# The opening of a two-layer trunk: squares and split pieces dealt out anew, the second scale units moved into the first products, no products of zeros

## Chip, cores and metric

One core of a Trainium2 chip. The metric is the device time of one execution in microseconds (us), the median over runs. The kernel before takes 1187.4 us (three runs, 1187.0 to 1189.1).

## What is computed

A trunk of two layers over 256 latent tokens and 256 context tokens of width 1024. Layer 0 is attention beside a convolution module, layer 1 banded attention beside a state-space mixer, each followed by a gated feed-forward network. All norms are modulated by shifts and scales that are themselves a product with the condition vectors. The opening, which is what the change touches, is this part:

```python
sh1, sc1, g1, sh2, sc2, g2 = jnp.split((jax.nn.silu(c) @ mod_w[l] + mod_b[l])[:, None, :], 6, axis=-1)
csh1, csc1, ... = jnp.split(jax.nn.silu(c_ctx) @ mod_w[l] + mod_b[l], 6)
h  = modulate(rms_norm(x,  norm1_g[l]), sh1, sc1)      # h * (1 + scale) + shift
hc = modulate(rms_norm(cx, norm1_g[l]), csh1, csc1)
q, k, v, glu = jnp.split(h @ w_in, cuts, axis=-1)      # even_mixer, layer 0
```

## The kernel before

Activations stand feature-major in SBUF: `X[:, f, :]` is feature tile f (0 to 7) by 512 tokens. A product of fp32 accuracy is made of three: weights and activations are split in a high part that the fast format holds (`w_hi`, `Hhi`) and the rest (`w_lo`, `Hlo`), and hi x hi, hi x lo and lo x hi are summed. Each weight block (8 tiles by 256 columns, 1 MB) comes by SyncE's queue into one of four slots `raw`; ScalarE makes `w_hi`, VectorE `w_lo`, in two halves of 1024 columns, and a slot is free when both halves of `w_lo` are made (semaphore `lo_split`). The stream of loads is a list: blocks 0 and 1, four loads of the shifts of `mod_w` (0, 0, k=4 to 7), block 2, and so on; load r goes to slot r mod 4. So shift loads 4 and 5 have slots 2 and 3 at once, and shift loads 6 and 7 must wait until the halves 1 of blocks 0 and 1 are split. SyncE issues in the order of the list and stands at each wait.

The order of the opening is written out by hand, engine by engine:

TensorE (`@block.tensor`): fourteen products of zeros, `cvec` with itself, into a bank nobody reads (L2011). Then 32 transposes of x, four for each f (L2006), with three transposes of the small vectors `vrow` behind f=3. Then the sums of squares, `first_sum(f)`, four small products each (L2101), with `mod_unit(0)` behind f=3; `mod_unit(1)`; the turn of the first scales `scales_T(0)` and `spread_roots`, which spreads 1/rms over the partitions (L2117); `mod_unit(2)` and `mod_unit(3)` (L2039). Units 0 and 1 give the first four tiles of scales, 2 and 3 the second four; each is 16 products of a condition vector with a load `first_mod[m]`. Then `first_two()`: the first two weight blocks. `column(b, j, m)` is the three products of block b, feature tile j and output half m. It goes through block 0 with j=0 to 3, block 1 with j=0 to 3, the shift units `mod_unit(4)` to `mod_unit(7)` (L2055), block 0 with j=4 to 7, and the rest. The turn of the second scales, `scales_T(1)`, stands ahead of j=3 of block 0.

VectorE (`@block.vector`): `turned(f)` copies the transposed tile out of PSUM for even f (ScalarE does it for odd f, L749), `square0(f)` squares f = 0, 2, 4, 6 (L1214), the reciprocal of the root (L1368), `scales_copy(0)` (L1241), `first_gains(0)`, which makes the gains from the turned scales (L1248, L1251); then `gained0(f)`, the normed tile `n_h0` in two halves (L1377), `low0(f)`, its rest `Hlo` (L1384), and `first_lo(w, part)` (L660), a half of `w_lo`. `first_gains(1)` stands ahead of `first_lo(0, 1)` and `first_lo(1, 1)`, and `gained0` for f=4 to 7 needs those gains.

ScalarE: `turned` for odd f; `vec_ready`, then silu of the condition vectors into `cvec` (L757); a table load; `turned(5)`, `turned(7)`; the squares 5 and 7 (L764); the root (L786); `first_high(f)`, which is `Hhi` (L791), and `first_hi(w, part)` (L654).

GpSimd: the squares 1 and 3 (L698), then `w_hi` and `w_lo` of the first half of block 0 (L701, L703), then `Hlo` of f = 2, 4, 6 (L713). A tiny `ptap` memset (L710) passes on the count for the tiles that VectorE makes.

SyncE: x and the context, small vectors, then in order `first_block(0, 0)`, `first_scales(0)`, `(1)`, `first_block(1, 0)`, `first_scales(2)`, `(3)`, `first_block(0, 1)`, `first_block(1, 1)`, and the list. The loads 0 and 1 of the scales count on one semaphore, on which `mod_unit(0)` waits for both; 2 and 3 have one each.

Of the kernel before, what the change touches and what calls it, by code (L numbers as in the profile page):

```python
# [26 lines left out]
P = 128  # L27
# [129 lines left out]
def build_trunk(nc, a, out):  # L157
    with ExitStack() as ctx:
# [156 lines left out]
        def s(name):  # L315
            if name not in S:
                S[name] = sem(name)
            return S[name]
# [6 lines left out]
        def tiles(w):  # L325
            return w.rearrange("(k p) n -> p k n", p=P)
# [144 lines left out]
        def _(sp):  # L471
# [5 lines left out]
            def first_scales(i):  # L477

                rows_, cols_ = 4 * P * (i % 2), P * SC1 + 4 * P * (i // 2)
                sp.dma_start(first_mod[i][:, :].rearrange("p (k n) -> p k n", k=4),  # L480
                             tiles(a["mod_w"][0, rows_:rows_ + 4 * P, cols_:cols_ + 4 * P])).then_inc(s(f"scales_loaded{max(i - 1, 0)}"), 16)

            def first_block(r, part, loaded):

# [171 lines left out]
        def first_lo(w, part):  # L656

            c0 = 1024 * part
            nc.vector.wait_ge(hi_split, FIRST[w, part])
            nc.vector.tensor_tensor(w_lo[:, w, c0:c0 + 1024], raw[:, w, c0:c0 + 1024], w_hi[:, w, c0:c0 + 1024].bitcast(F32),  # L660
                                    ALU.subtract).then_inc(lo_split, 1)
# [5 lines left out]
            return Cc[:, i - 10, :], lambda tap: XB[:, i, 0, tap:tap + LAT]  # L667

        LOW_DVE = (0, 1, 3, 5, 7)
        SQ_DVE, SQ_POOL, SQ_ACT = (0, 2, 4, 6), (1, 3), (5, 7)  # L670
        XS_BANK = (p5, pmod, p5, pmod, p7, p5, pmod, p7)
        OUT_BANK = ((p5, p6), (p7, pmod))
        X_TOK = ((0, 0, p7), (0, 1, p5), (1, 0, p6), (1, 1, p7))
# [18 lines left out]
        @block.gpsimd  # L692
        def _(pool):
            nc.gpsimd.memset(U[:, :, :, :], 0.0).then_inc(s("pads_A"), 1)

            for i, f in enumerate(SQ_POOL):
                pool.wait_ge(s("xT_act"), f // 2 + 1)
                nc.gpsimd.tensor_tensor(sq0[:, f, :], X[:, f, :], X[:, f, :], ALU.mult).then_inc(s("sq_pool"), 1)  # L698

            pool.wait_ge(s("first_rows0"), 16)  # L700
            nc.gpsimd.tensor_copy(w_hi[:, 0, 0:1024], raw[:, 0, 0:1024]).then_inc(hi_split, 1)  # L701
            pool.wait_ge(hi_split, 1)
            nc.gpsimd.tensor_tensor(w_lo[:, 0, 0:1024], raw[:, 0, 0:1024], w_hi[:, 0, 0:1024].bitcast(F32), ALU.subtract)\  # L703
                .then_inc(lo_split, 1)

            for f in range(KD):
                if f in LOW_DVE:

                    pool.wait_ge(s("h_lo_dve"), LOW_DVE.index(f) + 1)
                    nc.gpsimd.memset(ptap[:, f:f + 1], 0.0).then_inc(s("h_lo"), 1)  # L710
                    continue
                pool.wait_ge(s("h_hi"), f + 1)
                nc.gpsimd.tensor_tensor(Hlo[:, f, :], n_h0[:, f, :], Hhi[:, f, :].bitcast(F32), ALU.subtract)\  # L713
                    .then_inc(s("h_lo"), 1)

            pool.wait_ge(s("h_lo"), 3 * KD)
            nc.gpsimd.memset(XB[:, :, :, 0:2], 0.0).then_inc(s("pads_C"), 1)
            nc.gpsimd.memset(XB[:, :, :, 2 + LAT:4 + LAT], 0.0).then_inc(s("pads_C"), 1)
            pool.wait_ge(s("pads_C"), 2)
            pool.wait_ge(s("aux_done"), 6)  # L720
            nc.gpsimd.memset(Xb[:, 4:6, 2 * LAT:2 * T], 0.0).then_inc(s("parts_zero"), 1)
# [3 lines left out]
        def _(act):  # L725
# [34 lines left out]
            turned(5)  # L760
            turned(7)
            for f in SQ_ACT:
                act.wait_ge(s("xT_act"), f // 2 + 1)
                A(sq0[:, f, :], X[:, f, :], ACT.Square).then_inc(s("sq_ready"), 1)  # L764

            def root(n, t):
# [432 lines left out]
        def _(dve):  # L1199
# [11 lines left out]
            def square0(f):  # L1211

                dve.wait_ge(s("xT_dve"), f // 2 + 1)
                V_.tensor_tensor(sq0[:, f, :], X[:, f, :], X[:, f, :], ALU.mult).then_inc(s("sq_dve"), 1)  # L1214
# [8 lines left out]
            square0(2)  # L1223
            turned(6)
            square0(4)
            square0(6)

            GROUPS = [(l, j) for l in range(DEPTH) for j in range(3)]

# [8 lines left out]
            def scales_copy(i):  # L1238

                dve.wait_ge(mod_used, 2 * i + 2)  # L1240
                V_.tensor_copy(modc[:, 0:P], pmod[:, 0:P]).then_inc(s("modc_ready"), 1)  # L1241
# [139 lines left out]
            def low0(f):  # L1381

                dve.wait_ge(s("h_hi"), f + 1)
                V_.tensor_tensor(Hlo[:, f, :], n_h0[:, f, :], Hhi[:, f, :].bitcast(F32), ALU.subtract)\  # L1384
                    .then_inc(s("h_lo_dve"), 1)
# [3 lines left out]
            low0(0)  # L1389
            gained0(2)  # L1390
            low0(1)
            scales_copy(1)
            gained0(3)
            dve.wait_ge(lo_split, 1)
            first_lo(1, 0)
            low0(3)
            first_gains(1)
            first_lo(0, 1)
            first_lo(1, 1)
# [601 lines left out]
        def _(pe):  # L2001
# [4 lines left out]
                return nc.tensor.transpose(o, x, cst("ident", 0, n, 0, n))  # L2006


            pe.wait_ge(s("cvec_zero"), 2)
            for _ in range(14):  # L2010
                mm(p6[0:32, 0:KD * 32], cvec[:, 0, :], cvec[:, :, :].rearrange("p k c -> p (k c)"), start=True, stop=True)  # L2011

            pe.wait_ge(s("const_loaded"), 16)
            pe.wait_ge(s("x_loaded"), 32)
            for f in range(KD):
# [11 lines left out]
            def mod_unit(m):  # L2027

                n, k = m // KD, m % KD
                if m < 4:  # L2030
                    pe.wait_ge(s(f"scales_loaded{max(m - 1, 0)}"), 32 if m < 2 else 16)
                    if m == 0:
                        pe.wait_ge(s("cvec_ready"), 1)
                    if m == 2:
                        pe.wait_ge(s("gains_ready"), 1)
                    for kk in range(4 * (m % 2), 4 * (m % 2) + 4):
                        for g in range(4):
                            c0 = 4 * P * (kk % 4) + P * g
                            ins = mm(pmod[32 * g:32 * g + 32, 0:P], cvec[:, kk, :], first_mod[m][:, c0:c0 + P],  # L2039
                                     start=(kk == 0), stop=(kk == KD - 1))  # L2040
                    ins.then_inc(mod_used, 1)
                    return
                r = m_raw[m]
                pe.wait_ge(raw_loaded[r % RAW_SLOTS], 16 * (r // RAW_SLOTS + 1))
                if k == 0 and n:
                    pe.wait_ge(s("mod_ready"), n)
                if k == 0 and n == 1:
                    pe.wait_ge(s("shift_ready"), 1)
                if n == 0:
                    if k == 4:  # L2050
                        pe.wait_ge(s("mod_ready"), 1)
                    for kk in range(2 * (k % 4), 2 * (k % 4) + 2):
                        for g in range(4):
                            c0 = D * (kk % 2) + 256 * g
                            ins = mm(pmod[32 * g:32 * g + 32, 0:256], cvec[:, kk, :], raw[:, r % RAW_SLOTS, c0:c0 + 256],  # L2055
                                     start=(kk == 0), stop=(kk == KD - 1))
                    ins.then_inc(mod_used, 1)
                    return
                if k == 0 and n == 3:
                    pe.wait_ge(s("yn_ready"), BT)  # L2060
                if k == 0 and n == 5:
                    pe.wait_ge(s("decay_ready"), 16)
                if k == 4 and n == 5:
                    pe.wait_ge(s("mod_ready"), 6)
                if n == 5:
                    for kk in range(2 * (k % 4), 2 * (k % 4) + 2):
                        for g in range(4):
                            c0 = D * (kk % 2) + 256 * g
                            ins = mm(pmod[32 * g:32 * g + 32, 0:256], cvec[:, kk, :], raw[:, r % RAW_SLOTS, c0:c0 + 256],
                                     start=(kk == 0), stop=(kk == KD - 1))  # L2070
                else:
                    for g in range(4):
                        ins = mm(pmod[32 * g:32 * g + 32, :], cvec[:, k, :], raw[:, r % RAW_SLOTS, g * 512:(g + 1) * 512],  # L2073
                                 start=(k == 0), stop=(k == KD - 1))
                ins.then_inc(mod_used, 1)
# [8 lines left out]
            def scales_T(i):  # L2084

                pe.wait_ge(s("modc_ready"), i + 1)
                T_(pmod[:, 0:P], modc[:, 0:P]).then_inc(s("modT_done"), 1)
# [37 lines left out]
            mod_unit(1)  # L2125
            scales_T(0)
            spread_roots(0, T)
            mod_unit(2)
            mod_unit(3)

            def part_ready(w, part, it=None, per=0):

# [43 lines left out]
            def first_two():  # L2176
# [11 lines left out]
                pe.wait_ge(lo_split, FIRST[0, 0])  # L2188
                for j in range(4):
                    pe.wait_ge(s("h_lo_dve") if j < 2 else s("h_lo"), j + 1)  # L2190
                    if j == 3:
                        scales_T(1)
                    for m in range(2):
                        column(0, j, m)
                pe.wait_ge(lo_split, FIRST[1, 0])
                for j in range(4):
                    for m in range(2):
                        ins = column(1, j, m)
                ins.then_inc(s("h_used"), 1)
# [785 lines left out]
```

## Time and profile before

| | |
|---|---|
| median of 3 runs | 1187.4 us (1187.0 to 1189.1) |
| profiled execution | 1187.6 us |
| its span | 1185.8 us |
| TensorE busy | 1157.7 us, 98% |
| VectorE busy | 693.6 us, 58% |
| ScalarE busy | 485.3 us, 41% |
| GpSimd busy | 13.9 us, 1% |
| chain that ended last | PE 85%, DVE 10%, ACT 2%, DMA 2% |

Times in the rows are us from the start of the span. PE is TensorE, PEld its weight loads, DVE VectorE, ACT ScalarE, POOL GpSimd, SP SyncE; SPq is SyncE's queue while it issues. In a row of the timeline the bracket at the end is the idle time ahead of the piece and who ended it. Matmuls overlap: a record of TensorE is longer than the distance to the next. A product of the first blocks counts as one record, a small fp32 product as two.

### The profile page before, as it was taken

The page shows a single profiled execution, that of the slowest core. Times are in us where ns is not written, and L with a number is a line of the kernel's source. Part 1 is how long each engine was busy: PE and PEld are TensorE (multiplying, and loading weights), DVE is VectorE, ACT ScalarE, POOL GpSimd, SP SyncE. Part 2 cuts the span into 40 slices and gives each one's busy share as a digit, 9 for nine tenths or more (in the row PEclk, how much of TensorE's full clock was granted, in tenths as well). Part 3 has the DMA queues.
Part 4 walks back from the last instruction along what each step waited for, and adds up shares of the span by engine and source line. Part 5 has one row for each costly group of instructions (what it writes and reads, how often), then busy time and mean ns, then how long its engine had stood idle before and what let it go on. Part 6 is the DMA issues. An engine that isn't in the chain of part 4 may idle for free.

```text
span 1185.8 us, 17766 instructions
## 1 busy us (share of the span) xinstructions
PE 1157.7 (98%) x7266; PEld 934.1 (79%) x7266; DVE 693.6 (58%) x1159; ACT 485.3 (41%) x744; POOL 13.9 (1%) x20
## 2 busy tenths in 40 slices
PE   8999999999999999999999999999999999999998
PEld 5777766777588888888887767899565898998997
DVE  5699978853643334423323368887789645554455
ACT  3423336552433232222212242367268636443442
POOL 3000000000000000000000000000000000000000
PEclk9999999999999999999999999999999999999999
DMA  9845473125543222332123664344140157655551
GB/s 346 316 152 177 159 251 122 36 82 203 184 139 104 88 76 84 125 123 84 67 80 116 206 198 142 95 119 143 36 143 2 47 178 239 213 177 179 193 167 65
DMA packets 118893, 167.73 MB, mean 141 GB/s; under 512 B 4797, under 2 KB 102695, under 8 KB 114599
## 3 DMA queue, kind: packets, MB, share of 16 engines
q1 hardware_dynamic: 118390, 166.23, 42.1%
q8 instruction: 50, 0.82, 0.3%
q10 hardware_dynamic: 433, 0.51, 0.2%
q14 instruction: 20, 0.16, 0.0%
HBM read 164.37 MB, written 1.05 MB: 139 GB/s over the span
## 4 chain that ended last, share of the span: by engine, by line
PE 85%; DVE 10%; ACT 2%; DMA 2%; issue 1%; SPq 0%; DVEq 0%; ACTq 0%; POOL 0%
PE acc L2153 20%; PE acc L2154 20%; PE acc L2155 20%; PE pmod L2073 2%; PE acc L2232 2%; PE acc L2233 1%; PE acc L2234 1%; PE p L2518 1%; PE p L2519 1%; PE p L2517 1%; DMA first_mod<-in_mod_w 1%; PE p L2006 1%; DVE Y L1429 1%; DVE sm L1511 1%; PE p L2395 1%
## 5 line engine op out<-in xcount | busy, mean ns | idle before, releaser
L646 DVE TENSOR_TENSOR w_lo<-raw,w_hi 128x1024 fp32r<-128x1024 f32 x222 | 249.0, 1163 | 234.8 <-ACT w_hi L636 234.5
L636 ACT ACTIVATE w_hi<-raw 128x1024 fp32r<-128x1024 f32 (+1 forms) x224 | 212.8, 998 | 408.7 <-PE acc L2155 358.2
L2153 PE MATMUL acc<-Hhi,w_hi 128*128 128x512 f32 (+1 forms) x960 | 326.3, 340 | 1.6 <-DVE w_lo L646 1.6
L2155 PE MATMUL acc<-Hhi,w_lo 128*128 128x512 f32 (+1 forms) x960 | 324.3, 338 | 0.0
L2154 PE MATMUL acc<-Hlo,w_hi 128*128 128x512 f32 (+1 forms) x960 | 324.2, 338 | 0.0
L2153 PEld LDWEIGHTS acc<-Hhi,w_hi 128*128 128x128 f32 x960 | 182.1, 190 | 25.7 <-issue 3.9
L2155 PEld LDWEIGHTS acc<-Hhi,w_lo 128*128 128x128 f32 x960 | 182.1, 190 | 19.6
L2154 PEld LDWEIGHTS acc<-Hlo,w_hi 128*128 128x128 f32 x960 | 182.2, 190 | 19.2
L2153 PE MATMUL acc<-hid_hi,w_hi 128*128 128x512 f32 x248 | 97.9, 395 | 0.1
L2154 PE MATMUL acc<-hid_lo,w_hi 128*128 128x512 f32 x248 | 96.6, 390 | 0.0
L2155 PE MATMUL acc<-hid_hi,w_lo 128*128 128x512 f32 x248 | 96.6, 389 | 0.0
L1429 DVE SCALAR_TENSOR_TENSOR Y<-U,vec,Y 128x512 f32<-128x512 f32 x120 | 82.0, 746 | 0.3
L1654 DVE TENSOR_TENSOR f_h<-acc,f_gate 128x1024 f32<-128x1024 f32 (+1 forms) x22 | 21.1, 958 | 102.2 <-PE acc L2155 100.2
L2153 PEld LDWEIGHTS acc<-hid_hi,w_hi 128*128 128x128 f32 x248 | 46.5, 188 | 13.9 <-issue 3.5
L2155 PEld LDWEIGHTS acc<-hid_hi,w_lo 128*128 128x128 f32 x248 | 46.6, 188 | 9.9
L2154 PEld LDWEIGHTS acc<-hid_lo,w_hi 128*128 128x128 f32 x248 | 46.6, 188 | 9.2
L1608 DVE SCALAR_TENSOR_TENSOR X<-acc,mod,X 128x256 f32<-128x256 f32 (+1 forms) x52 | 22.0, 478 | 40.5 <-PE acc L2155 40.5
L2232 PE MATMUL acc<-Hhi,w_hi 128*128 128x512 f32 (+1 forms) x96 | 35.4, 369 | 2.1 <-DVE Hlo L1353 2.1
L2153 PE MATMUL acc<-mixC_hi,w_hi 128*128 128x256 f32 x128 | 36.7, 287 | 0.0
L2154 PE MATMUL acc<-mixC_lo,w_hi 128*128 128x256 f32 x128 | 36.2, 283 | 0.0
L2155 PE MATMUL acc<-mixC_hi,w_lo 128*128 128x256 f32 x128 | 36.2, 283 | 0.0
L2073 PE MATMUL pmod<-raw,cvec 128*32 128x512 f32 x256 | 33.2, 602 | 1.2 <-DVE small L1327 1.2
(392 smaller groups left out, 1602.8 us busy)
## 6 DMA issues: line engine op xcount, KB each, us to landing
raw<-in_mod_w SPq DMA_DIRECT2D x44, 1024.0 KB, 5.3
raw<-in_ffn_w_in SPq DMA_DIRECT2D x44, 1024.0 KB, 5.1
raw<-in_od_w_in SPq DMA_DIRECT2D x15, 1024.0 KB, 5.4
raw<-in_ffn_w_out SPq DMA_DIRECT2D x12, 768.0 KB, 4.5
raw<-in_ev_w_in SPq DMA_DIRECT2D x8, 1024.0 KB, 7.5
raw<-in_od_w_out SPq DMA_DIRECT2D x8, 1024.0 KB, 5.9
raw<-in_ffn_w_out SPq DMA_DIRECT2D x8, 1024.0 KB, 5.0
raw<-in_ev_w_out SPq DMA_DIRECT2D x8, 768.0 KB, 6.3
```

The source lines that it names most:

```text
L636: nc.scalar.activation(w_hi[:, w % 2, c0:c1], raw[:, r % RAW_SLOTS, c0:c1], ACT.Copy)\
L646: nc.vector.tensor_tensor(w_lo[:, w % 2, c0:c1], raw[:, r % RAW_SLOTS, c0:c1], w_hi[:, w % 2, c0:c1].bitcast(F32), ALU.subtract).then_inc( ...
L1429: ins = V_.scalar_tensor_tensor(out=y, in0=U[:, i, :, tap:tap + LAT], scalar=col, in1=y, op0=ALU.mult, op1=ALU.add)
L1511: top = step.mark(V_.reduce_max(sm[:, v % 3, 0:1], sbank[v % 3][:, nk_of(v)[0] * P:T], AX.X))
L1608: ins = V_.scalar_tensor_tensor(out=xs, in0=src, scalar=gt, in1=xs, op0=ALU.mult, op1=ALU.add)
L1654: V_.tensor_tensor(f_h[:, :, 0:t], acc[:, 2:4, 0:t], f_gate[:, :, 0:t], ALU.mult)\
L2006: return nc.tensor.transpose(o, x, cst("ident", 0, n, 0, n))
L2073: ins = mm(pmod[32 * g:32 * g + 32, :], cvec[:, k, :], raw[:, r % RAW_SLOTS, g * 512:(g + 1) * 512], start=(k == 0), stop=(k == KD - 1))
L2153: mm(outs[m], hi[:, j, cols], xh, start=(first and j == 0), stop=False)
L2154: mm(outs[m], hi[:, j, cols], xl, start=False, stop=False)
L2155: ins = mm(outs[m], lo[:, j, cols], xh, start=False, stop=(last and j == kts - 1))
L2232: mm(o, hi[:, j, cols], xh, start=(j == 0), stop=False)
```

## The change

Seven edits, all in the opening:

1. The fourteen products of zeros are gone.
2. The square of f=6 moves from VectorE to ScalarE, between 5 and 7.
3. GpSimd makes only `w_hi` of the first half of block 0; `w_lo` of it, `first_lo(0, 0)`, goes to VectorE, into the place of the square of f=6. VectorE's wait for GpSimd's piece ahead of `first_lo(1, 0)` goes with it.
4. Scale loads 0 and 1 get a semaphore each, 2 and 3 share one; `mod_unit(0)` waits only for load 0, units 2 and 3 for both of theirs.
5. `mod_unit(2)` and `mod_unit(3)` move from ahead of `first_two()` to ahead of j=2 of block 0.
6. `scales_T(1)` moves from ahead of j=3 of block 0 to ahead of j=1 of block 1.
7. `scales_copy(1)` on VectorE moves from ahead of `gained0(3)` to behind `low0(3)`.

```diff
@@ first_scales
-  ... .then_inc(s(f"scales_loaded{max(i - 1, 0)}"), 16)
+  ... .then_inc(s(f"scales_loaded{min(i, 2)}"), 16)
@@
-        SQ_DVE, SQ_POOL, SQ_ACT = (0, 2, 4, 6), (1, 3), (5, 7)
+        SQ_DVE, SQ_POOL, SQ_ACT = (0, 2, 4), (1, 3), (5, 6, 7)
@@ GpSimd
             nc.gpsimd.tensor_copy(w_hi[:, 0, 0:1024], raw[:, 0, 0:1024]).then_inc(hi_split, 1)
-            pool.wait_ge(hi_split, 1)
-            nc.gpsimd.tensor_tensor(w_lo[:, 0, 0:1024], raw[:, 0, 0:1024], w_hi[:, 0, 0:1024].bitcast(F32), ALU.subtract)\
-                .then_inc(lo_split, 1)
@@ ScalarE
             for f in SQ_ACT:
-                act.wait_ge(s("xT_act"), f // 2 + 1)
+                act.wait_ge(s("xT_act") if f % 2 else s("xT_dve"), f // 2 + 1)
@@ VectorE
             square0(4)
-            square0(6)
+            first_lo(0, 0)
@@
             low0(1)
-            scales_copy(1)
             gained0(3)
-            dve.wait_ge(lo_split, 1)
             first_lo(1, 0)
             low0(3)
+            scales_copy(1)
             first_gains(1)
             first_lo(0, 1)
             first_lo(1, 1)
@@ TensorE
-            pe.wait_ge(s("cvec_zero"), 2)
-            for _ in range(14):
-                mm(p6[0:32, 0:KD * 32], cvec[:, 0, :], cvec[:, :, :].rearrange("p k c -> p (k c)"), start=True, stop=True)
@@ mod_unit
-                    pe.wait_ge(s(f"scales_loaded{max(m - 1, 0)}"), 32 if m < 2 else 16)
+                    pe.wait_ge(s(f"scales_loaded{min(m, 2)}"), 16 if m < 2 else 32)
@@
             spread_roots(0, T)
-            mod_unit(2)
-            mod_unit(3)
@@ first_two
                 for j in range(4):
                     pe.wait_ge(s("h_lo_dve") if j < 2 else s("h_lo"), j + 1)
-                    if j == 3:
-                        scales_T(1)
+                    if j == 2:
+                        mod_unit(2)
+                        mod_unit(3)
                     for m in range(2):
                         column(0, j, m)
                 pe.wait_ge(lo_split, FIRST[1, 0])
                 for j in range(4):
+                    if j == 1:
+                        scales_T(1)
                     for m in range(2):
                         ins = column(1, j, m)
```

TensorE's order from the second scale unit to the first products, before (`first_mod_90` to `_92` are the loads of units 1 to 3, `acc` the first products, `Hhi` and `w_hi` their high parts):

```order
L2101 MATMUL p<-sq_93,const 32x128 x16
L2039 MATMUL pmod<-first_mod_90,cvec 32x128 x16
L2006 MATMUL pmod<-const,modc 128x128
L2117 MATMUL p<-rs_95,const 128x128 x4
L2039 MATMUL pmod<-first_mod_91,cvec 32x128 x16
L2039 MATMUL pmod<-first_mod_92,cvec 32x128 x16
L2184 MATMUL acc<-Hhi,w_hi 128x512
```

The same place in the changed kernel:

```order
L2092 MATMUL p<-sq_93,const 32x128 x16
L2030 MATMUL pmod<-first_mod_90,cvec 32x128 x16
L2001 MATMUL pmod<-const,modc 128x128
L2108 MATMUL p<-rs_95,const 128x128 x4
L2173 MATMUL acc<-Hhi,w_hi 128x512
```

The two units stand twelve products further down, and the next `pmod<-const,modc` (the turn of the second scales) thirty products and the two units behind the first `acc`, where before it was eighteen products behind it.

VectorE's order from the first products' second tile to the tiles from 4 on, before, with what each row waits for:

```order
L1384 TENSOR_TENSOR Hlo<-n_h_76,Hhi 128x512 [waits h_hi]
L1241 COPY modc<-pmod 128x128 [waits mod_used]
L1377 SCALAR_TENSOR_TENSOR n_h_76<-X,gain,p 128x256 x2
L660 TENSOR_TENSOR w_lo<-raw,w_hi 128x1024 [waits hi_split,lo_split]
L1384 TENSOR_TENSOR Hlo<-n_h_76,Hhi 128x512 [waits h_hi]
L1248 TENSOR_TENSOR mod<-pmod,vec 128x8 [waits modT_done]
L1251 SCALAR_TENSOR_TENSOR gain<-mod,vec 128x8 [waits dve_step]
L660 TENSOR_TENSOR w_lo<-raw,w_hi 128x1024 [waits hi_split,mod_ready]
L660 TENSOR_TENSOR w_lo<-raw,w_hi 128x1024 [waits hi_split]
```

And in the changed kernel:

```order
L1380 TENSOR_TENSOR Hlo<-n_h_76,Hhi 128x512 [waits h_hi]
L1373 SCALAR_TENSOR_TENSOR n_h_76<-X,gain,p 128x256 x2
L660 TENSOR_TENSOR w_lo<-raw,w_hi 128x1024 [waits hi_split]
L1380 TENSOR_TENSOR Hlo<-n_h_76,Hhi 128x512 [waits h_hi]
L1237 COPY modc<-pmod 128x128 [waits mod_used]
L1244 TENSOR_TENSOR mod<-pmod,vec 128x8 [waits modT_done]
L1247 SCALAR_TENSOR_TENSOR gain<-mod,vec 128x8 [waits dve_step]
L660 TENSOR_TENSOR w_lo<-raw,w_hi 128x1024 [waits hi_split,mod_ready]
L660 TENSOR_TENSOR w_lo<-raw,w_hi 128x1024 [waits hi_split]
```

The copy of the second scales now stands directly ahead of the gains made from them; the last two `w_lo` are behind both, as before.

## Rows read from the trace of the kernel before

**Rows 1.** The page, busy time of TensorE over the whole span.

```profile
PE 1157.7 (98%) x7266; PEld 934.1 (79%) x7266; DVE 693.6 (58%) x1159; ACT 485.3 (41%) x744; POOL 13.9 (1%) x20
```

**Rows 2.** Chain of waits, 0 to 43 us: start, length, what.

```profile
24.20 1.66 DVE n_h L1377 x4
25.85 0.61 DVE Hlo L1384
...
31.25 0.34 PE pmod L2006
...
32.02 2.37 DVE w_lo L660 x2
34.41 6.80 DMA raw<-in_mod_w
...
41.24 1.07 PE pmod L2055 x16
...
43.21 0.23 PE acc L2184
```

**Rows 3.** Timeline of TensorE: start, length, instructions, pause ahead of them.

```profile
1.24 8.03 PE L2011 MATMUL p<-cvec 128*32 128x256 f32 x28 [1.24 <-DVE cvec L1205]
10.17 1.94 PE L2006 MATMUL acc<-const,xin 128*128 128x128 f32 x16 [0.91 <-DMA xin<-in_ctx]
...
16.08 0.64 PE L2101 MATMUL p<-sq,const 128*32 128x128 f32 x16 [1.10 <-DVE sq L1214]
17.95 1.39 PE L2039 MATMUL pmod<-first_mod,cvec 128*32 128x128 f32 x32 [1.23 <-DMA first_mod<-in_mod_w]
...
25.66 1.08 PE L2039 MATMUL pmod<-first_mod,cvec 128*32 128x128 f32 x32 [0.57 <-DMA first_mod<-in_mod_w]
...
38.34 3.98 PE L2055 MATMUL pmod<-raw,cvec 128*32 128x256 f32 x64
```

**Rows 4.** SyncE's waits, and the landings of its four shift loads (L517).

```profile
SPq L517 <- DVE w_lo L660: 11.2, 2, 10.4
DMA to landing us min/median/max: 5.4/9.1/12.4
```

**Rows 5.** Groups of TensorE from 1.2 to 5 us, and from 5 to 9.3.

```profile
L2011 PE MATMUL p<-cvec 128*32 128x256 f32 x9 | 3.9, 621 | 1.2 <-DVE cvec L1205 1.2
L2011 PE MATMUL p<-cvec 128*32 128x256 f32 x20 | 4.6, 386 | 0.0
```

**Rows 6.** Timeline of VectorE, 11 to 20 us.

```profile
11.71 0.69 DVE L1209 COPY X<-acc 128x512 f32<-128x512 f32 x1 [0.18 <-PE acc L2006]
...
13.52 0.52 DVE L1220 COPY vec<-p 128x364 f32<-128x364 f32 x1
...
15.15 0.87 DVE L1214 TENSOR_TENSOR sq<-X 128x512 f32<-128x512 f32 x1
...
16.55 2.86 DVE L1214 TENSOR_TENSOR sq<-X 128x512 f32<-128x512 f32 x2
```

**Rows 7.** Timeline of ScalarE, 14 to 22 us.

```profile
14.08 0.22 ACT L757 ACTIVATE cvec<-vec 128x16 f32<-128x16 f32 x1 [1.34 <-DVE vec L1220]
...
16.82 1.15 ACT L764 ACTIVATE sq<-X 128x512 f32<-128x512 f32 x2
21.10 0.37 ACT L786 ACTIVATE rt<-p,small 128x128 f32<-128x128 f32 x1 [3.13 <-PE p L2101]
```

**Rows 8.** Timeline of GpSimd, 15 to 30 us.

```profile
15.56 2.69 POOL L703 TENSOR_TENSOR w_lo<-raw,w_hi 128x1024 fp32r<-128x1024 f32 x1
...
28.07 1.29 POOL L713 TENSOR_TENSOR Hlo<-n_h,Hhi 128x512 fp32r<-128x512 f32 x1
```

**Rows 9.** Stretches: from:to, length, TensorE busy, granted clock, DMA share, GB/s.

```profile
15.00:18.60 3.60, 1.29 (x40) 1.00 1.07 371
18.60:22.00 3.40, 3.40 (x72) 0.50 1.05 385
32.50:33.00 0.50, 0.50 (x4) 1.00 0.12 49
```

More of the change, by code:

```diff
@@ L480, in first_scales @@
                 sp.dma_start(first_mod[i][:, :].rearrange("p (k n) -> p k n", k=4),
-                             tiles(a["mod_w"][0, rows_:rows_ + 4 * P, cols_:cols_ + 4 * P])).then_inc(s(f"scales_loaded{max(i - 1, 0)}"), 16)
+                             tiles(a["mod_w"][0, rows_:rows_ + 4 * P, cols_:cols_ + 4 * P])).then_inc(s(f"scales_loaded{min(i, 2)}"), 16)
             def first_block(r, part, loaded):
```

## The prediction

> **What bounds the kernel now.** I read the page first: of a span of 1185.8 us TensorE is busy 98% [rows 1]. So the whole program is one long TensorE queue, and a change in the opening matters by how far it moves the moment from which that queue no longer starves. The chain of waits for the first 43 us says what that moment hangs on [rows 2]. It reaches back to the loads of the first scales, for which TensorE waits until 17.95 [rows 3]; then come four sums of squares, the second unit, the copy and the turn of the scales, and at 24.20 VectorE makes the first `n_h`. From there the chain stays on VectorE until the turn of the second scales at 31.25, goes on with the last two halves of `w_lo` (32.02 to 34.39), and these free the slots of the raw ring: the transfer issued at 34.41 lands 6.80 later, and the last shift unit runs from 41.24 to 42.31. Behind that TensorE follows without a gap, a product each 0.23. So two things set the time at which the opening ends: TensorE's own work, and the last transfer, which waits for VectorE. TensorE's queue in order of time shows them nearly level, since the four shift units run 38.34 to 42.32, four times about one us, with no room for a wait [rows 3]. SyncE's queue shows the other side: it waited 11.2 us for exactly those two `w_lo` pieces [rows 4].
>
> **The change, part by part.** Times are of the profiled execution, 1187.6 us (span 1185.8 and 1.8 around it), 0.2 over the median of the three runs, 1187.4; I add the difference to the median.
>
> *No products of zeros.* They end at 9.27 and TensorE's first transpose waits for x until 10.17 anyway [rows 3], so no time of theirs is on the path. What they bought is the clock. The first nine of them take 3.76 us (1.24 to 5.0), 0.42 each; the next twenty take 4.3, 0.21 each [rows 5]. The engine's clock thus rose from 1.2 to 2.4 GHz at about 5 us, after 3.8 us of back-to-back work. In the changed kernel the transposes are the first work, so they meet the lower clock. The rule behind it is in the Trainium skill, "TensorE: Matmul & The Clock Gate", section "What's actually happening": the throttled state is the default and activity releases it; the first rows of zeros agree.
> Sixteen transposes take 1.94 at full clock [rows 3], 0.11 each with 0.16 for the tail; at half clock 0.22. The tile of f=2 is then turned at 10.17 + 12 x 0.22 + 0.16 = 12.97, VectorE copies it (0.69) and squares f=0 (0.87 at least), and copies `vec` after that, starting at about 14.7 where it was 13.52 [rows 6]. ScalarE's silu of `cvec` waits for that copy: 15.2 for 14.08 [rows 7]. Behind it stand, in ScalarE's order, a table load, two copies and the squares; from silu to the end of its two squares took 3.89 (14.08 to 17.97).
>
> *Sixth square on ScalarE.* A third square adds 0.57 there: 15.24 + 3.89 + 0.57 = 19.7. On VectorE the square of f=4 ends near 18.5 and the moved `first_lo(0, 0)` near 19.7. For the squares I take 0.87, the duration of the one at 15.15, and not the 1.43 of the two at 16.55: those ran beside GpSimd's subtraction of 15.56 to 18.25, which is removed [rows 6, 8]. The Trainium skill, "SBUF — State Buffer", on which operations grab the shared pair, says that a VectorE operation with two inputs in SBUF contends with GpSimd's reads; the longer squares agree. At the contended durations VectorE would be free about 0.2 later than the root needs it, and the sum would be larger by that 0.2. I keep ScalarE as the later one.
> The last sum then ends at about 20.1, for 21.05. From the root (21.10) to the first `n_h` (24.20) is 3.10 [rows 2, 7]. The second scale unit fits: 20.1 + 1.08 is before the reciprocal ends. So `n_h` starts at 20.15 + 3.10 = 23.25: a **gain of 0.95**. Its bounds: no cost of the low clock at all, 18.95 + 0.05 + 3.10 = 22.1, a gain of 2.1; low clock through the sums, the turn and the spreading of the roots (0.5 + 0.4 + 1.0 more), a loss of 0.9.
>
> *The splitting of the wait on the two scale loads* lets unit 0 start before 17.95. It stands ahead of sums that wait for later squares, so I cost it at nothing; its cover is ScalarE's squares up to 19.7.
>
> *Second scale units behind the second tile.* In the kernel before the second of them ran from 25.66 to 26.74, and the first ahead of it, while TensorE would have had nothing to do but wait for `Hlo` until 26.46 [rows 2, 3]. Now they stand in the dense part: 1.08 + 0.84, say 1.9 for the pair. Worse is what they push back, the turn of the second scales. Counted from the start of `n_h`: the first tile product can start at +2.26 (26.46 - 24.20); j=2 waits 0.15 for GpSimd's subtraction (28.07 + 1.29 = 29.36, +5.16 for +5.02) [rows 8]; the turn now has ahead of it j=0 to 3 of block 0 and j=0 of block 1, five times six products at 0.23 = 6.9, and the pair, 1.9. It is issued at +11.2, where it was at +7.05 (31.25): **4.15 later**, less the gain of 0.95, **3.2 later**, at 34.45. VectorE stands in `first_gains(1)` for it, doing nothing from about 29.5, with `first_lo(0, 1)` and `first_lo(1, 1)` queued behind, both of which had their input long before. SyncE waits for those with the two loads of the ring, and the DMA engines have been idle since about 32 (0.12 busy from 32.5 on) [rows 9]. So the second load is issued at 34.41 + 3.2 = 37.6 and lands at 44.4; unit 7 ends near 45.5 where it ended at 42.31. VectorE's later squares of work (`n_h` 4 to 7, Hlo) move by the same 3.2 and stay ahead of it. TensorE's own sum is smaller: 23.25 + 2.26 + 0.15 + 1.9 + 0.33 + 8 x 1.38 + 4 x 1.0 = 42.9, only 0.6 late; what decides is the load. TensorE reaches unit 6 at 40.9, finds its load landed at about 33.24 + 3.2 + 5.4 = 41.8 (5.4 is the shortest of the four landings [rows 4]), and then waits 1.6 for unit 7.
>
> *The clock once more.* Units 2 and 3 no longer fill TensorE's pause before the first tile: after the roots are spread (23.25) it has nothing until `Hlo` at 25.5, and it had a pause before the turn as well. From 15.0 to 18.6 TensorE was busy 1.29, in short pieces between pauses of 1.10 and 1.23, and at 18.65 the clock fell to 1.2 GHz for 3.4 us, until 22.06 [rows 3, 9]. The new pauses are of that kind: 1.1 ahead of the first turn (20.9 to 22.0), 1.3 of work, and 2.2 ahead of the first tile. A fall costs half of what it covers of dense products, at most 1.7, about **1.4** with the part that lies in the pause. The second pause, around units 6 and 7, can do the same.
>
> Sum: 3.2 + 1.4 = 4.6, nothing being absorbed later: up to 58 us TensorE has no pause, and its waits behind that are for VectorE and ScalarE work that moves along. **1187.4 + 4.6 = 1192.0 us.**
>
> **The rivals.** (a) The clock holds: only the load is late, 1187.4 + 3.2 = 1190.6. For it: after 22.06 the clock held over the pause of 0.57 ahead of unit 3 [rows 3]. (b) The clock falls at both pauses: 3.2 + 1.4 + 1.6 = 6.2, 1193.6. For it: around units 6 and 7 TensorE is busy only 2 in 4.6 us. (c) The head gains its full 2.1, because ScalarE's chain isn't held by the low clock: the turn is late by 4.15 - 2.1 = 2.05, and 1189.5 comes out. Against it: `vec` stands behind nineteen transposes. (d) The other side: the load is no longer the bound, at the place where unit 7 waits. TensorE's own sum decides then, and with a gain of 2.1 it is 0.6 - 1.15 = -0.55: 1186.9 or a bit less. It decides from the point where the last load takes less than 4.3 us (issued at 36.45, wanted at 40.8). Against it: the same load took 6.80, and none of the four under 5.4. (e) The change does nothing, since the scales were late by a transfer anyway: the chain has no transfer between 17.95 and 34.41, so this gets nearly nothing; it would be 1187.4.
>
> **How the numbers follow.** A measurement of this kernel tells about 0.2% (2.4 us) from no change. My case with one fall 0.36, (a) 0.20, (b) 0.17: these are slower by more than 0.2%, 0.73 together. (c) 0.14 and (e), with a part of the delay absorbed in a way I don't see, 0.06: within 0.2%, 0.20. (d) and gains I don't see, 0.07. The likeliest gives 1192.0. The range goes from 1188.4, which takes in (c) with a little absorbed, to 1194.4, (b) with 0.8 for a gain near nothing.
>
> **What would show it.** In the changed profile: the transposes at twice 0.11 each; silu near 15.2; three squares on ScalarE ending near 19.7; the first `n_h` near 23.2; VectorE idle about 5 us in front of the second `first_gains`, with the turn near 34.5; SyncE's wait for `w_lo` up from 11.2 to 14 or so; a transfer issued near 37.6 and TensorE waiting for it before unit 7; first tile products twice as long for up to 3.4 us if the clock falls. The prediction is wrong if unit 7 ends before 44, or if something behind 60 us gives time back.

## The result and the profile after

| | before | changed |
|---|---|---|
| median | 1187.52 us (6 runs, 1186.73 to 1189.1) | 1192.76 us (6 runs, 1192.06 to 1193.56) |
| profiled execution | 1187.6 us | 1192.4 us |
| its span | 1185.8 us | 1190.6 us |

The changed kernel takes 1.0044 of the time before, 95% interval 1.0031 to 1.0057: 5.2 us more by the medians, 4.8 by the profiled executions. The forecast was 1192.0.

The page, busy time by engine. It answers to [rows 1]: TensorE is busy 5.9 less, and its span is 4.8 longer.

```profile
PE 1151.8 (97%) x7238; PEld 932.9 (78%) x7238; DVE 692.4 (58%) x1159; ACT 485.9 (41%) x745; POOL 10.8 (1%) x19
```

The chain of waits of the changed kernel, 20 to 47 us (start, length, what), against [rows 2]:

```profile
20.18 0.38 ACT rt L782
20.58 0.95 DVE rs L1364
...
23.07 1.66 DVE n_h L1373 x4
...
29.91 1.98 PE pmod L2030 x64
36.21 0.12 PE pmod L2001
36.36 0.18 DVE mod L1244
...
36.76 2.37 DVE w_lo L660 x2
39.15 6.90 DMA raw<-in_mod_w
46.09 1.07 PE pmod L2046 x16
```

`n_h` starts 1.13 earlier (23.07 for 24.20). Between it and the turn of the second scales the chain has another path: before, it stayed on VectorE up to the turn at 31.25 [rows 2]; now, behind the first `Hlo`, it runs over TensorE's own products and the pair of units. From the turn on the members and their order are the same. `w_lo` starts 4.74 later (36.76 for 32.02), the transfer behind it is issued at 39.15 for 34.41, also 4.74 later, and unit 7 ends at 47.16 for 42.31, 4.85 late. The spans differ by 4.8, so nearly all of the loss is made in the 13 us between the first `n_h` and the second gains, and none of it is given back later.

TensorE's timeline of the changed kernel (start, length, instructions, and the pause ahead of them), against [rows 3]:

```profile
10.37 3.65 PE L2001 MATMUL acc<-const,xin 128*128 128x128 f32 x16 [10.37 <-DMA xin<-in_ctx]
...
29.84 2.05 PE L2030 MATMUL pmod<-first_mod,cvec 128*32 128x128 f32 x64
36.05 0.27 PE L2001 MATMUL pmod<-const,modc 128*128 128x128 f32 x1
40.38 1.93 PE L2046 MATMUL pmod<-raw,cvec 128*32 128x256 f32 x32
43.19 1.07 PE L2046 MATMUL pmod<-raw,cvec 128*32 128x256 f32 x16 [0.88 <-DMA raw<-in_mod_w]
46.09 1.07 PE L2046 MATMUL pmod<-raw,cvec 128*32 128x256 f32 x16 [1.83 <-DMA raw<-in_mod_w]
```

The four shift units, one row of 3.98 before, are now three pieces with two pauses for loads between them. The pauses stand where TensorE's queue touches the ring; read alone, they would say "the memory is slow". VectorE's timeline says whose fault they are:

```profile
29.23 0.68 DVE L1380 TENSOR_TENSOR Hlo<-n_h,Hhi 128x512 fp32r<-128x512 f32 x1
31.97 0.29 DVE L1237 COPY modc<-pmod 128x128 f32<-128x128 f32 x1 [2.06 <-PE pmod L2030]
36.36 0.17 DVE L1244 TENSOR_TENSOR mod<-pmod,vec 128x8 f32<-128x8 f32 x1 [4.10 <-PE pmod L2001]
```

Between `low0(3)` and the second gains VectorE is idle for 2.06 and 4.10 us, with two `w_lo` pieces queued behind that need nothing from either wait. SyncE's waits (engine, line, total us, times, longest), against the 11.2 of [rows 4]:

```profile
SPq L517 <- DVE w_lo L660: 15.3, 2, 14.5
```

And the stretches (from:to, length, TensorE busy, granted clock, DMA share, GB/s), for the clock, against [rows 9]:

```profile
23.00:26.50 3.50, 1.02 (x5) 1.00 1.08 359
26.50:30.00 3.50, 3.50 (x13) 0.53 1.04 407
42.00:45.50 3.50, 1.38 (x24) 1.00 1.00 382
46.50:50.00 3.50, 3.50 (x28) 1.00 1.09 411
```

Behind the pause ahead of the first tile the clock is at 1.2 GHz from 26.7 to 30.1: 13 records in 3.5 us of dense products. Behind the pauses at units 6 and 7 it holds in this execution.

### The profile page after: what moved, and what is told of

It reads as the page before. It is cut to its first block, busy times and chain, and to the rows that moved or that the text cites. A ratio compares the mean times of both kernels' runs of the same rounds, so it can differ in the third digit from the quotient of the medians.

```text
span 1190.6 us, 17708 instructions
## 1 busy us (share of the span) xinstructions
PE 1151.8 (97%) x7238; PEld 932.9 (78%) x7238; DVE 692.4 (58%) x1159; ACT 485.9 (41%) x745; POOL 10.8 (1%) x19
## 4 chain that ended last, share of the span: by engine, by line
PE 86%; DVE 9%; ACT 2%; DMA 1%; issue 1%; SPq 0%; DVEq 0%; ACTq 0%
PE acc L2142 20%; PE acc L2144 20%; PE acc L2143 20%; PE pmod L2064 2%; PE acc L2224 2%; PE acc L2226 1%; PE acc L2225 1%; PE p L2511 1%; PE p L2509 1%; PE p L2510 1%; PE acc L2001 1%; PE p L2001 1%; DVE Y L1424 1%; DVE sm L1506 1%; DMA xin<-in_ctx 1%
```

## The experiments

My theory at this point: 3.3 us come from the late transfers, which wait for VectorE, which waits for the turn; 1.5 from the fall of the clock in the pause ahead of the first tile. Rivals: TensorE's own sum with the units in the dense part decides (the loads don't matter), or the missing zeros and ScalarE's third square cost time themselves. Each comparison below is with the kernel before on the same chip, whose median lay between 1187.4 and 1188.1.

### The late halves of `w_lo` ahead of the wait

```diff
             low0(3)
+            first_lo(0, 1)
+            first_lo(1, 1)
             scales_copy(1)
             first_gains(1)
-            first_lo(0, 1)
-            first_lo(1, 1)
```

> The changed kernel with the last two halves of w_lo ahead of the copy and the gains of the second scales on VectorE, so that they no longer wait for the turn at 36.05. If the late transfers decide, SyncE issues them near 31 and 32, they land before TensorE asks, the two pauses ahead of units 6 and 7 (0.88 and 1.83) go, unit 7 ends near 44.4 instead of 47.16, and the time is 1192.8 - 2.8 = 1190.0 us. If TensorE's own work and its clock decide instead, it stays within 0.5 us of 1192.8.

Measured: 1189.68 us (10 runs), 1.0012 of before, interval 1.0002 to 1.0021. The first row is VectorE's timeline, the second TensorE's:

```profile
29.76 2.35 DVE L660 TENSOR_TENSOR w_lo<-raw,w_hi 128x1024 fp32r<-128x1024 f32 x2
```

```profile
40.41 3.66 PE L2046 MATMUL pmod<-raw,cvec 128*32 128x256 f32 x64
```

The pieces are made at 29.8 for 36.8, the shift units are one row again, and unit 7 ends at 44.07 for 47.16, though the turn itself is where it was (36.08). By the medians the excess over the kernel before is 1.6 where it was 5.2. So 3.1 us (unit 7 in the traces) to 3.7 (the excesses) were the late transfers, and TensorE's own sum isn't what decided in the changed kernel.

### The turn itself earlier

```diff
@@ first_two, in the changed kernel
                     if j == 2:
                         mod_unit(2)
                         mod_unit(3)
+                    if j == 3:
+                        scales_T(1)
@@ block 1
-                    if j == 1:
-                        scales_T(1)
```

> The changed kernel with the turn of the second scales ahead of j=3 of block 0, directly behind units 2 and 3 and one tile, instead of ahead of j=1 of block 1. If the place of the turn is what delays the last two loads, the turn is 2.8 earlier (33.3), both pauses at units 6 and 7 go, and the time falls by 2.5 to 3 us against the changed kernel, to the kernel before plus 2 to 2.5; the units themselves may stay where they are. If the units' place is what costs, the time stays at plus 4.5 to 5.

Measured: 1189.73 us (10 runs), 1.0018 of before (1.0008 to 1.0027), plus 1.9. The turn came at 34.50 and not at 33.3, because the clock stayed low for 6.8 us in this execution, but both pauses at the units are gone:

```profile
34.50 0.27 PE L2001 MATMUL pmod<-const,modc 128*128 128x128 f32 x1
41.52 3.82 PE L2046 MATMUL pmod<-raw,cvec 128*32 128x256 f32 x64
```

Two different edits, one on VectorE and one on TensorE, cut the same chain and end at the same 1189.7. What they have in common is that the last loads are issued in time. That the medians agree so closely is partly chance: unit 7 ended at 45.34 here and at 44.07 in the run before, since the clock was low for longer, and that run had another fall of the clock later on (last section).

### TensorE's pause filled

```diff
             spread_roots(0, T)
+            for _ in range(5):
+                mm(p7[0:32, 0:KD * 32], cvec[:, 0, :], cvec[:, :, :].rearrange("p k c -> p (k c)"), start=True, stop=True)
```

> The changed kernel with five idle products of cvec, as large as the products of zeros, between the spreading of the roots and the first tile; their result is read by nobody. If the pause there lets the clock fall, the granted clock now stays at 2.4 GHz from 26 to 31 and the turn is 1.5 earlier, near 34.6: 1191.2 us. If the fall has another cause, 1192.8 or a little more.

Measured: 1192.67 us (4 runs, 1190.79 to 1193.69), 1.0044 of before (1.0027 to 1.006). The profiled execution is the 1190.79 one; its stretches:

```profile
23.00:26.50 3.50, 3.25 (x15) 1.00 1.09 362
26.50:30.00 3.50, 3.50 (x73) 1.00 1.05 408
```

In the trace it is as expected: the clock stays at 2.4 GHz, 73 records in the second stretch where the changed kernel has 13, the turn at 34.38 for 36.05, and the span 1189.0 for 1190.6. The other three executions were 1.4 to 2.9 us longer, and the median does not move. The pauses of 0.88 and 1.85 at units 6 and 7 are still in this kernel. Their mean granted clock was lower, 0.997 to 0.999 for the 1.000 of the profiled one, and the slower the execution, the lower it was. So the clock was low for longer in them; in which place isn't shown, since there is no trace of them.

### Both mends

```diff
@@ VectorE
             low0(3)
+            first_lo(0, 1)
+            first_lo(1, 1)
             scales_copy(1)
             first_gains(1)
-            first_lo(0, 1)
-            first_lo(1, 1)
@@ TensorE
             spread_roots(0, T)
+            for _ in range(5):
+                mm(p7[0:32, 0:KD * 32], cvec[:, 0, :], cvec[:, :, :].rearrange("p k c -> p (k c)"), start=True, stop=True)
```

> The changed kernel with both mends: the last two halves of w_lo ahead of the copy and gains, and five idle products in the pause ahead of the first tile. If late loads and the fall of the clock are the whole of the loss and add up, the first takes 2.8 and the second 1.5 of it, and the kernel before plus 0.3 to 0.8 us is left, which is the 1.9 of the pair of units less the gain of the head. If a third cause is left, plus 1.5 or more.

Measured: 1187.58 us (11 runs, 1187.3 to 1188.2), 0.9999 of before (0.999 to 1.0008). Expected were 0.3 to 0.8 over before, which the interval still takes in; a third cause of 1.5 or more is excluded. So the two causes together make up the loss, within about 1 us. Part of the difference between -0.2 and the expected 0.3 to 0.8 can be the clock: eight of the eleven executions had a mean granted clock of 1.000, but only eight of the 21 of the kernel before, and between these two groups of eight the kernel with both mends is slower, 1187.5 for 1187.1 in the mean. In TensorE's timeline the whole of it can be seen, with no pause in the units, and unit 7 ending at 42.39 where it ended at 42.31:

```profile
22.76 2.35 PE L2120 MATMUL p<-cvec 128*32 128x256 f32 x10
28.30 1.96 PE L2030 MATMUL pmod<-first_mod,cvec 128*32 128x128 f32 x64
34.40 0.27 PE L2001 MATMUL pmod<-const,modc 128*128 128x128 f32 x1
38.73 3.66 PE L2046 MATMUL pmod<-raw,cvec 128*32 128x256 f32 x64
```

Without the mend of the pause the excess over before was 1.6, and here it is -0.2, so the pause costs 1.8 by the medians, about one fall of the clock; by the ends of unit 7 it is 1.68 (44.07 and 42.39).

### The move alone, and the zeros alone

```diff
@@ the kernel before
             spread_roots(0, T)
-            mod_unit(2)
-            mod_unit(3)
@@ first_two
-                    if j == 3:
-                        scales_T(1)
+                    if j == 2:
+                        mod_unit(2)
+                        mod_unit(3)
@@ block 1
+                    if j == 1:
+                        scales_T(1)
@@ VectorE
-            scales_copy(1)
             gained0(3)
             dve.wait_ge(lo_split, 1)
             first_lo(1, 0)
             low0(3)
+            scales_copy(1)
```

> The kernel before with nothing but the move of units 2 and 3, of the turn and of the copy of the second scales; zeros, squares, GpSimd's piece and the semaphores as before. If the move is the cause by itself, the first tile stays near 26.5, the turn is 4.3 to 5.8 late (35.5, or 37 where the clock falls in the pause from 24.1 to 26.5), TensorE waits ahead of units 6 and 7, and the time is the kernel before plus 4.3 to 7 us. If the head's edits are the cause, plus less than 1.

Measured: 1196.71 us (4 runs), 1.008 of before (1.0064 to 1.0095), plus 9.3: more than the upper end of what I expected. Its timeline of TensorE and a stretch:

```profile
40.48 1.93 PE L2055 MATMUL pmod<-raw,cvec 128*32 128x256 f32 x32
43.35 1.07 PE L2055 MATMUL pmod<-raw,cvec 128*32 128x256 f32 x16 [0.93 <-DMA raw<-in_mod_w]
47.11 1.93 PE L2055 MATMUL pmod<-raw,cvec 128*32 128x256 f32 x16 [2.69 <-DMA raw<-in_mod_w]
```

```profile
45.50:49.00 3.50, 1.89 (x17) 0.61 1.10 392
49.00:52.50 3.50, 3.50 (x12) 0.50 1.01 420
```

The turn was at 36.17, inside the expected 35.5 to 37, and the last load was issued at 39.27. But it took 7.80 to land, not 6.80, and the clock fell in the pause of 2.69, so that unit 7 and what follows ran at 1.2 GHz until about 53. Ahead of the first tile, on the other hand, TensorE had a pause of 2.52 here too, and the clock held:

```profile
23.00:26.50 3.50, 1.22 (x9) 1.00 1.09 361
26.50:30.00 3.50, 2.87 (x12) 1.00 1.03 403
```

So this is not rival (b) as it was written, with a fall at both pauses, but its second fall alone. The move by itself costs 4 us more than the whole change. That is not because the other edits had won 4: the head gained 1.65 (first `n_h` at 24.72 here, 23.07 in the changed kernel), which the fall in the first pause took back, so that the turn came at 36.17 and 36.05. The rest is made behind the turn, by a load that took 0.9 longer and by the second fall.

```diff
@@ the kernel before
-            pe.wait_ge(s("cvec_zero"), 2)
-            for _ in range(14):
-                mm(p6[0:32, 0:KD * 32], cvec[:, 0, :], cvec[:, :, :].rearrange("p k c -> p (k c)"), start=True, stop=True)
```

> The kernel before without the products of zeros. Transposes at 1.2 GHz, silu near 15.2, first n_h 0 to 0.7 later than 24.20; units 2 and 3 and the load of unit 3 (25.66) cover most of it, and units in the pauses hold the clock: kernel before plus 0 to 0.5 us. If the missing zeros let the clock fall ahead of the first tile, plus 1.5 or more.

Measured: 1187.67 us (10 runs), 1.0004 of before (0.9994 to 1.0013): no difference that can be told. The first sixteen transposes take 3.54 for 1.94, but behind them the clock holds through the sums, where it fell at 18.65 before [rows 9], and the first `n_h` came at 23.95, even a bit earlier than 24.20.

### The zeros put back into the changed kernel

```diff
+            pe.wait_ge(s("cvec_zero"), 2)
+            for _ in range(14):
+                mm(p6[0:32, 0:KD * 32], cvec[:, 0, :], cvec[:, :, :].rearrange("p k c -> p (k c)"), start=True, stop=True)
+
             pe.wait_ge(s("const_loaded"), 16)
```

> The changed kernel with the fourteen products of zeros put back. Transposes at 2.4 GHz, silu near 14.1, first n_h near 22.1 instead of 23.07; pause before the first tile unchanged in length, so the clock still falls there, and the turn comes 1.0 earlier: 1191.8 us. If the zeros had kept the clock up through the pause too, 1190.3. If the missing zeros cost nothing, 1192.8.

Measured: 1195.66 us (4 runs), 1.0065 of before (1.0048 to 1.0082). I had the sign wrong: 7.6 over before for the changed kernel's 5.2, so the zeros make it slower by 2.4 and not faster by 1.0. The head did as expected, silu at 14.32, first `n_h` at 22.17, turn at 35.19. Then:

```profile
38.30 7.96 DMA raw<-in_mod_w
46.26 0.04 issue
46.30 1.94 PE pmod L2050 x16
```

```profile
42.00:45.50 3.50, 1.07 (x16) 0.95 1.03 393
46.50:50.00 3.50, 3.50 (x20) 0.50 1.06 413
```

The load was issued 0.85 earlier and landed 0.21 later than in the changed kernel, the pause was 2.74, and the clock fell in it. It had fallen in the first pause as well (low from about 24.7 to 28), so this is rival (b) of the prediction seen whole in a trace. The earlier head gained nothing because the load took 1.06 longer, and the longer pause in front of it went with a second fall. Why this transfer took 6.8 to 6.9 us in five traces and 7.8 to 8.0 in two, this and the move alone, stays open.

### The units back, and which semaphores

The changed kernel with the units, the turn and the copy at their old places:

```diff
             spread_roots(0, T)
+            mod_unit(2)
+            mod_unit(3)
@@ first_two
-                    if j == 2:
-                        mod_unit(2)
-                        mod_unit(3)
+                    if j == 3:
+                        scales_T(1)
@@ block 1
-                    if j == 1:
-                        scales_T(1)
@@ VectorE
             low0(1)
+            scales_copy(1)
             gained0(3)
             first_lo(1, 0)
             low0(3)
-            scales_copy(1)
```

> The changed kernel with units 2 and 3, the turn and the copy of the second scales back at their places of before; the other edits stay. If the move of the units is the cause, this gives all of it back: first tile product near 26.7 (unit 3 waits for its load until about 25.7), turn near 31.2, unit 7 ends near 42.3, time 1187.5 us plus or minus 0.4. If the missing products of zeros or ScalarE's third square cost time themselves, it stays over 1189.

Measured: 1189.7 us (10 runs), 1.0017 of before (1.0008 to 1.0027). It gave back 3.6 us of the excess, but not all. The reason stands in one row: with the semaphore shared by loads 2 and 3, unit 2 waits for load 3 as well, and the clock falls in the pause, so that the pair takes 3.49.

```profile
25.68 3.49 PE L2030 MATMUL pmod<-first_mod,cvec 128*32 128x128 f32 x64 [2.47 <-DMA first_mod<-in_mod_w]
```

I had costed the split of the semaphores at nothing, which holds only where the units stand late. The same kernel with the old semaphores:

```diff
-  ... .then_inc(s(f"scales_loaded{min(i, 2)}"), 16)
+  ... .then_inc(s(f"scales_loaded{max(i - 1, 0)}"), 16)
@@
-                    pe.wait_ge(s(f"scales_loaded{min(m, 2)}"), 16 if m < 2 else 32)
+                    pe.wait_ge(s(f"scales_loaded{max(m - 1, 0)}"), 32 if m < 2 else 16)
```

> The changed kernel with units 2 and 3, the turn and the copy back at their places, and the semaphores of the scale loads as before, so that unit 2 doesn't wait for load 3. It differs from the run with the units back by the semaphores alone. If the shared semaphore made the pause of 2.47 in which the clock fell there, unit 2 now runs near 23.5, the pause is 1 to 1.6, the clock holds, unit 7 ends near 42.3: kernel before plus 0 to 0.5 us. If not, it stays at plus 1.6 to 2.

Measured: 1187.12 us (10 runs, 1186.48 to 1187.45), 0.9995 of before (0.9986 to 1.0005). Unit 2 runs in the pause and the clock holds:

```profile
23.05 1.08 PE L2030 MATMUL pmod<-first_mod,cvec 128*32 128x128 f32 x32
25.30 1.08 PE L2030 MATMUL pmod<-first_mod,cvec 128*32 128x128 f32 x32 [1.17 <-DMA first_mod<-in_mod_w]
```

This is what the head's edits are worth without the move: 0.3 us by the medians, inside the noise. In its trace the turn is at 30.54 for 31.25 and unit 7 ends at 41.53 for 42.31, so 0.8 at most; no more, because unit 3 still waits for its load until 25.3.

### A version to beat both

The changed kernel with zeros, the late halves of `w_lo` ahead of the wait, the old semaphores, and three idle products and unit 2 in the pause.

```diff
             spread_roots(0, T)
+            for _ in range(3):
+                mm(p7[0:32, 0:KD * 32], cvec[:, 0, :], cvec[:, :, :].rearrange("p k c -> p (k c)"), start=True, stop=True)
+            mod_unit(2)
@@ first_two
                     if j == 2:
-                        mod_unit(2)
                         mod_unit(3)
```

> The changed kernel with the zeros put back, the last two halves of w_lo ahead of the copy and gains of the second scales, the semaphores of the scale loads as before, and in TensorE's pause ahead of the first tile three idle products and unit 2; unit 3 alone stays ahead of j=2. First tile near 24.5, clock at 2.4 GHz from about 5 us on, no wait ahead of units 6 and 7, unit 7 ends near 40.9 for 42.3: kernel before minus 1.4 us. If the opening is bound by something else by then, no better than before.

Measured: 1188.16 us (11 runs, 1186.8 to 1189.37), 1.0006 of before (0.9997 to 1.0015): a miss. In the trace unit 7 ended at 41.7 for 42.31, 0.6 earlier and not 1.4, because unit 0 waited for both first loads until 18.26, and `n_h` began at 23.18, not 22.2. The runs lie from 1186.8 to 1187.4 and from 1188.2 to 1189.4, 1.5 or so apart, which is the size of one fall of the clock. The mean granted clock was 0.999 to 1.000 in the five of the lower group and 0.997 to 0.999 in the six of the upper; the profiled one, of the lower group, had no fall in the opening. None of the kernels run here is clearly faster than the one before.

## Why the prediction was right

**The head** came as worked out. ScalarE's silu at 15.22 (15.2 said), its third square ending at 17.96 + 1.67 = 19.63 (19.7), the last sum before the root at 20.18 (20.1), the first `n_h` at 23.07 (23.25): a gain of 1.13, not 0.95. VectorE was free at 19.63 and waited 0.95 for the root, so leaving the 1.43 of the contended squares out of the sum was right. But the 0.87 that the prediction took in their place wasn't a duration alone: that square, at 15.15, began while GpSimd still copied `w_hi` (14.45 to 15.48). Alone a square takes 0.68 (17.81 in the changed kernel). The two that took 2.86 [rows 6] show what GpSimd does to them: they ended at 19.41, 1.16 after GpSimd's subtraction had ended at 18.25 [rows 8], which is two squares at 0.68 less the overlap of their records. So these durations fit a VectorE that stands until GpSimd is done and then runs at its own speed, rather than one that runs slower. The changed kernel has this once more, with a piece of `w_lo` that alone takes 1.22:

```profile
26.94 1.28 POOL L709 TENSOR_TENSOR Hlo<-n_h,Hhi 128x512 fp32r<-128x512 f32 x1
27.42 1.89 DVE L660 TENSOR_TENSOR w_lo<-raw,w_hi 128x1024 fp32r<-128x1024 f32 x1
```

It ended at 29.31, 1.09 after GpSimd's 28.22. The same piece in the kernel before ended at 30.44, 1.08 after GpSimd's 29.36. This agrees with the Trainium skill, "SBUF — State Buffer", section "Who interferes with whom": a VectorE instruction with two inputs in SBUF contends with a GpSimd instruction that reads SBUF.

**The low clock on the transposes** was right in size, 3.65 for 1.94, and it cost the head 0.9: with the zeros back `n_h` started at 22.17 for 23.07. The Trainium skill, "TensorE: Matmul & The Clock Gate", section "What's actually happening", says that the default is the throttled state; that these transposes, the first work of TensorE, ran at half speed agrees with it. But the zeros bought nothing in the end. Without them the kernel before took the same time, and with them the changed one took 2.4 more, through the longer load and the second fall.

**The pushed-back turn** was the main term, right in mechanism: 34.45 said with the clock held, 35.85 with it fallen (34.45 and the 1.4 of the fall); measured were 34.38 in the run with the pause filled and 36.05 in the changed kernel. Each of the two mends of its consequence took 3.3 to 3.7 us off the excess, where 3.2 was the term.

**The last load.** The issue was said for 37.6 with the clock held, so 39.0 with the 1.4 of the fall, and came at 39.15; it took 6.90 for 6.80; pauses of 0.9 and 1.6 said, 0.88 and 1.83 measured; unit 7 ending 4.6 late said, 4.85 measured.

**The clock in the pause.** The fall cost about 1.5: filling the pause brought the turn from 36.05 to 34.38, 0.14 of which is an earlier `n_h`. The pause was 2.53, not 2.2. That a fall would come here was a chance in the prediction (0.36 and 0.17), argued from one earlier fall; the same pause, 2.52 long, went without one in the run with the move alone. Rival (b), the second fall, does not show in the changed kernel's trace either, though it does in two of the experiments' traces, behind pauses of 2.69 and 2.74 where the changed kernel had 1.83. So the mechanism was right and that the number lies so near the case with exactly one fall is partly luck. Of the changed kernel's six runs three lie at 1192.1 to 1192.4 and three at 1193.1 to 1193.6, these with a mean granted clock of 0.997 for 0.999. So some executions had one fall more; where is open. This second group is why the median is 0.8 over the forecast.

**What was not seen.** Edit 4 was costed at nothing. For its second half, the semaphore shared by loads 2 and 3, that is so in the changed kernel, since the units stand behind load 3. But the two runs with the units back show that it costs 1.9 us (1.6 over before, and 0.3 under it) as soon as they don't. Its first half, unit 0 no longer waiting for load 1, was worth something: with the old semaphores unit 0 stood until 18.33 and 18.26 and the first `n_h` came at 23.24 (units and semaphores back) and 23.18 (zeros as well), for 23.07 and 22.17 with the new ones. That is 0.2 without the zeros and 1.0 with them.

**Rival (d)** did not come: the last load took 6.8 to 8.0 in every chain that goes through it, never under 4.3. What it says would remain without that bound was measured in the run with both mends, where the loads are issued in time: TensorE's own sum, with unit 7 ending at 42.39. The prediction's sum for it was 42.9. That is no gain over the 42.31 of before, since the 1.9 of the pair in the dense part eats the head's 1.1 and the pause that unit 3's wait had made.

## What to carry to other kernels

When a step moves down one engine's queue, count what else waits for its result: here a 0.3 us transpose held VectorE for 4.1 us, and behind it stood two operations that needed nothing from it but that alone freed the slots of the ring. Order a queue so that what frees buffers stands ahead of what waits. And work that fills a pause costs nothing there and its full length in the dense part; taking it out can also cost a fall of the clock, here in four of the five kernels that had the pause of 2.52 or 2.53 us ahead of the first tile. So an edit that empties a pause must be costed with that fall too, as a chance and not as a certainty.

## What the runs showed of the hardware

The same pause does not always bring a fall of the clock. Five traces have TensorE idle for 2.52 or 2.53 us ahead of the first tile: the clock fell in this pause or within 1.2 us behind it in the changed kernel, in the runs with `w_lo` or the turn moved and in the one with the zeros back, and it held in the run with the move alone. The low stretch was 3.4 us long in three of these, and 6.8 in the run with the turn moved.

The clock falls far from the change too, and not in every kernel's trace. In the run with the late halves of `w_lo` moved it fell again some 280 us later, in the attention, where nothing was changed:

```profile
310.00:315.00 5.00, 4.17 (x32) 0.72 0.49 154
```

In the profiled execution of the kernel before it held there. A fall between 310 and 323 is in the traces of four of the experiments' kernels and missing in the others. Even the executions of one kernel on one chip differ by it: of the 27 of the kernel before beside the run with the move alone, the twelve with a mean granted clock of 1.000 took 1186.9 in the mean, the eight with 0.999 took 1187.5 and the seven with 0.998 took 1188.0. So an edit in the opening worth under 1 us can't be told from this in ten runs.
